# Three experts instead of two gathered by rank, and the second half of the slot gather placed behind the third gate/up product

## The reference

```python
def hier_moe(h, w_rg, b_rg, w_re, b_re, w_gate, w_up, w_down):
    ...
    gate = grp_p[:, None] * jax.nn.softmax(top_val, axis=-1)
    expert = grp[:, None] * MOE_EXPERTS_PER_GROUP + top_idx
    ...
    def run_block(args):
        xb, e = args
        hid = jax.nn.silu(xb @ w_gate[e]) * (xb @ w_up[e])
        return hid @ w_down[e]

    ys = lax.map(run_block, (xs, blk_expert)).reshape(n_slots, D)
    out = jnp.zeros((T + 1, D), jnp.float32).at[slot_tok].add(
        ys.astype(jnp.float32) * slot_gate[:, None])[:T]
```

## Time and profile before

| | us |
|---|---|
| median of 3 runs | 1012.68 (1011.05 to 1013.63) |
| the profiled execution | 1009.09 |
| its span in the trace | 1007.3 |
| PE busy | 928.9 (92%) |
| DVE busy | 277.3 (28%) |
| ACT busy | 205.7 (20%) |
| POOL busy | 184.3 (18%) |

### The profile page before, as it was taken

The page is one execution under the profiler, slowest core; times in us unless marked ns, Lnnn a source line. Parts: engine busy times, 40 slices in busy tenths (PEclk is TensorE's granted clock), DMA queues, the critical chain, the costliest instruction groups (busy, mean ns, idle before and its releaser), DMA issues.

```text
span 1007.3 us, 13643 instructions
## 1 busy us (share of the span) xinstructions
PE 928.9 (92%) x5416; PEld 555.1 (55%) x5416; DVE 277.3 (28%) x732; ACT 205.7 (20%) x483; POOL 184.3 (18%) x307
## 2 busy tenths in 40 slices
PE   5899898999999999888898889799999889999886
PEld 4788686554444434343343334587677448488632
DVE  2399633411110011100100110233353145042214
ACT  2354323310000000000000000311126311012630
POOL 0177200121111111110110110001012102013313
PEclk8999999999999999999999999999999999999998
DMA  9995864589999999999999999922002942302001
GB/s 371 430 427 218 365 273 176 243 319 428 426 427 429 429 426 429 427 426 428 428 426 427 429 426 430 420 91 112 18 2 115 396 168 84 132 35 85 1 1 42
DMA packets 21949, 286.17 MB, mean 284 GB/s; under 512 B 2434, under 2 KB 3202, under 8 KB 4354
## 3 DMA queue, kind: packets, MB, share of 16 engines
q1 hardware_dynamic: 21168, 283.99, 67.7%
q10 hardware_dynamic: 722, 1.33, 0.3%
HBM read 284.26 MB, written 1.05 MB: 283 GB/s over the span
## 4 chain that ended last, share of the span: by engine, by line
PE 69%; DMA 24%; DVE 2%; POOL 2%; issue 1%; ACT 1%; SPq 1%; POOLq 0%; ACTq 0%; DVEq 0%
DMA arena<-in_w_expert_up 21%; PE bank L914 20%; PE bank L1122 14%; PE bank L1291 6%; PE bank L1139 5%; DMA arena<-in_w_glu 3%; PE bank L1254 3%; PE bank L1401 3%; PE bank L1149 3%; PE bank L1278 2%; PE bank L1110 1%; PE bank L981 1%; PE bank L1268 1%; PE bank L933 1%; PE bank L1325 1%
## 5 line engine op out<-in xcount | busy, mean ns | idle before, releaser
L1122 PE MATMUL bank<-arena 128*64 128x512 f32 x1024 | 226.1, 593 | 24.7 <-DMA arena<-in_w_expert_up 24.7
L914 PE MATMUL bank<-arena 128*128 128x256 f32 (+1 forms) x912 | 203.4, 384 | 6.8 <-ACT arena L788 4.3
L914 PEld LDWEIGHTS bank<-arena 128*128 128x128 f32 (+1 forms) x912 | 173.6, 191 | 34.6 <-issue 6.9
L1122 PEld LDWEIGHTS bank<-arena 128*64 128x64 f32 x1024 | 79.4, 137 | 167.8 <-issue 167.6
L1139 PE MATMUL bank<-arena 128*64 128x512 f32 x512 | 116.9, 598 | 0.8 <-ACT arena L758 0.8
L1700 DVE TENSOR_TENSOR arena<-bank,arena 64x512 f32<-64x512 f32 x32 | 21.8, 682 | 280.1 <-ACT arena L754 280.1
L758 ACT ACTIVATE arena<-bank 128x512 f32<-128x512 f32 x32 | 19.1, 598 | 387.1 <-PE bank L1131 387.1
L1139 PEld LDWEIGHTS bank<-arena 128*64 128x64 f32 x512 | 34.1, 136 | 65.8 <-issue 65.8
L1149 PE MATMUL bank<-arena 64*128 64x256 f32 x512 | 65.8, 386 | 0.8 <-DVE arena L1703 0.8
L533 POOL COPY der<-arena 128x4 f32 (+1 forms) x30 | 5.6, 187 | 319.3 <-PE bank L1131 297.8
L1506 DVE SCALAR_TENSOR_TENSOR bank<-arena,par,bank 128x256 f32<-128x256 f32 x152 | 61.9, 483 | 0.6
(11 more groups left out here) (237 smaller groups left out, 847.2 us busy)
## 6 DMA issues: line engine op xcount, KB each, us to landing
arena<-in_w_expert_gate SPq DMA_DIRECT2D x32, 2048.0 KB, 27.1
arena<-in_w_expert_up SPq DMA_DIRECT2D x32, 2048.0 KB, 31.5
arena<-in_w_expert_down SPq DMA_DIRECT2D x32, 2048.0 KB, 30.8
arena<-in_w_ada SPq DMA_DIRECT2D x11, 2048.0 KB, 30.0
arena<-in_w_glu SPq DMA_DIRECT2D x4, 2048.0 KB, 34.8
arena<-in_w_kv SPq DMA_DIRECT2D x4, 2048.0 KB, 18.9
arena<-in_w_in_b SPq DMA_DIRECT2D x4, 2048.0 KB, 7.9
arena<-in_w_uq SPq DMA_DIRECT2D x4, 1152.0 KB, 13.9
```

Source lines behind the costliest of these rows:

```text
L914: mm = pe.matmul(bank[part:part + m, at:at + n], w[:, k, lo:lo + m], rhs[:, k0 + k, :], start=(k == 0), stop=(k == tiles - 1))
L1122: mm = pe.matmul(GU_BANK[half * WIN:(half + 1) * WIN, :], xw[b][:, k, :], w[:, k, :], start=(k == 0), stop=(k == KD - 1), skip_group_check ...
```

## The change

The gather by rank now covers three experts (BODY): DVE builds selectors of 192 columns instead of 128, the 16 matmuls are 192 columns wide instead of 128, and ACT moves 128 x 192 instead of 128 x 128. POOL prepares the weighting of experts 0, 1 and 2 at once (`first_window`) and no longer copies a window for expert 2.

The second half of the slot gather moves from behind gate/up 1 to behind gate/up 2. In between now stand the turn and down product of expert 0. The bank table follows: half 0 uses banks 1 to 7 from bank 1 on, half 1 uses banks 3 to 7. There are two waits for moves on PE as before, but each now stands directly behind a gather: for banks 1 to 3 behind half 0, ahead of gate/up 1, and for banks 4 to 7 behind half 1, ahead of finish(2). The turned buffer of expert 0 moves out of the memory of `sel`. ACT and DVE get the matching order.

```diff
-        for half in range(2):
-            for j in range(KD):
-                plan(("gather", half, j), 1 + (KD * half + j + 5) % 7)
+        for j in range(KD):
+            plan(("gather", 0, j), 1 + j % 7)
+        BEFORE_GATHER = list(reads)
+        for j in range(KD):
+            plan(("gather", 1, j), 3 + j % 5)
...
-            first_window(0)
-            first_window(1)
+            for e in range(BODY):
+                first_window(e)
             for half in range(2):
                 for j in range(KD):
                     moved(pool, ("gather", half, j))
-            window(2, 0, 2, win_ready)
...
-                    mm = pe.matmul(bank[:, 0:2 * WIN], h2_tok[:, t, j * P:(j + 1) * P], first_sel[:, t, :],
+                    mm = pe.matmul(bank[:, 0:BODY * WIN], h2_tok[:, t, j * P:(j + 1) * P], first_sel[:, t, :],
...
-                if e < 2:
-                    gather(e)
+                if e == 0:
+                    gather(0)
+                    for b in range(1, 4):
+                        pe.wait_ge(sem(f"bank{b}_read"), BEFORE_GATHER[b])
+                if e == 2:
+                    gather(1)
+                    for b in range(4, 8):
+                        pe.wait_ge(sem(f"bank{b}_read"), BEFORE_EXPERTS[b])
                 if e:
-                    for b in range(1, 4) if e == 1 else range(4, 8):
-                        pe.wait_ge(sem(f"bank{b}_read"), BEFORE_EXPERTS[b])
                     finish(e, e, lambda s, back: EXPERT_BASE[s] + 16, second=e == 1, third=e == 2)
...
-            for half in range(2):
-                for j in range(1, KD, 2):
-                    gathered(half, j)
-            with dve.Fori(1, EXPERTS) as e:
+            for j in range(1, KD, 2):
+                gathered(0, j)
+            dve.wait_ge(silu_done, 2)
+            dve.wait_ge(t_full, 1 + C_T)
+            gated(hid_ready)
+            dve.wait_ge(y_full, 1)
+            move_result(y_moved)
+            for j in range(1, KD, 2):
+                gathered(1, j)
+            with dve.Fori(2, EXPERTS) as e:
```

More of the change, by code:

```diff
@@ L143, in two_blocks @@
         wr2 = area(R + 6144, KD, CHOICES)
-        first_sel = area(R + 6144, NT, 2 * WIN)
+        first_sel = area(R + 6144, NT, BODY * WIN)
         shift_row, shift_all = small[0:1, 940:940 + CHOICES], small[:, 900:900 + CHOICES]
@@ L151, in two_blocks @@
         xw = [area(R + 4608 + b * KD * WIN, KD, WIN) for b in range(BODY)]
-        first_xw = arena[:, R + 4608:R + 4608 + 2 * KD * WIN].rearrange("p (e k n) -> p e k n", e=2, k=KD)
+        first_xw = arena[:, R + 4608:R + 4608 + BODY * KD * WIN].rearrange("p (e k n) -> p e k n", e=BODY, k=KD)
         weighted = [area(R + 12288 + b * NT * P, NT, P) for b in range(BODY)]
@@ L155, in two_blocks @@
         hid = arena[0:WIN, R + 6144:R + 6144 + HIDDEN]
-        turned_e = [arena[:, R + 10240 + b * 512:R + 10752 + b * 512] for b in range(BODY)]
+        turned_e = [arena[:, at:at + 512] for at in (R + 11264, R + 10240, R + 10752)]
         hid_t = [a[:, 0:KF * WIN].rearrange("p (f n) -> p f n", f=KF) for a in turned_e]
@@ L742, in _ @@
                 bank = filled(act, name)
-                act.activation(first_xw[:, :, j, :], bank[:, 0:2 * WIN].rearrange("p (e n) -> p e n", e=2), ACT.Identity,
+                act.activation(first_xw[:, :, j, :], bank[:, 0:BODY * WIN].rearrange("p (e n) -> p e n", e=BODY), ACT.Identity,
                                bias=mod[:, 24 + j:25 + j], scale=a2[:, j:j + 1]).then_inc(read(name), 1)
@@ L763, in _ @@
             silu(gu_full, 2, silu_done)
+            move_turned(t_full, C_T + 1, 0, t_moved)
+            silu(gu_full, 3, silu_done)
             for j in range(0, KD, 2):
                 gathered(1, j)
[L766 to L769, removed]
+            move_turned(t_full, C_T + 2, 1, t_moved)
+            silu(gu_full, 4, silu_done)
+            move_turned(t_full, C_T + 3, 2, t_moved)
             with act.Fori(1, LOOPS) as it:
@@ L1640, in _ @@
             iota = rc[:, R_IOTA:R_IOTA + SLOTS_A]
-            first_rank = tmp(990, NT, 2)
-            then(dve.scalar_tensor_tensor(out=first_rank, in0=bank[:, 0:64].rearrange("p (t e) -> p t e", t=NT)[:, :, 0:2],
-                                          scalar=1.0, in1=picked[:, :, 0:2], op0=ALU.add, op1=ALU.mult))
+            first_rank = tmp(990, NT, BODY)
+            then(dve.scalar_tensor_tensor(out=first_rank, in0=bank[:, 0:64].rearrange("p (t e) -> p t e", t=NT)[:, :, 0:BODY],
+                                          scalar=1.0, in1=picked[:, :, 0:BODY], op0=ALU.add, op1=ALU.mult))
             for t in range(NT):
-                dve.tensor_tensor(first_sel[:, t, :].rearrange("p (e n) -> p e n", e=2),
-                                  iota[:, 1:WIN + 1].unsqueeze(1).broadcast_to((P, 2, WIN)),
-                                  first_rank[:, t, :].unsqueeze(2).broadcast_to((P, 2, WIN)), ALU.is_equal) \
+                dve.tensor_tensor(first_sel[:, t, :].rearrange("p (e n) -> p e n", e=BODY),
+                                  iota[:, 1:WIN + 1].unsqueeze(1).broadcast_to((P, BODY, WIN)),
+                                  first_rank[:, t, :].unsqueeze(2).broadcast_to((P, BODY, WIN)), ALU.is_equal) \
                     .then_inc(sem("first_sel"), 1)
```

## The result

| | before | after |
|---|---|---|
| median of 20 runs each, us | 1011.08 (1006.38 to 1013.63) | 1013.83 (1009.43 to 1016.57) |
| ratio, 95% interval | | 1.0031 (1.0020 to 1.0043) |
| the profiled execution, us | 1009.09 | 1016.17 |
| its span | 1007.3 | 1014.4 |
| PE busy, us | 928.9 | 936.5 |

The change costs 3.1 us, between 2.0 and 4.3. The two medians differ by 2.75 us. The prediction had +1.3. A second timing of the changed kernel, beside the first experiments, gave 1.0025 (1.0006 to 1.0043).

The account below looks back on a forecast made before the run. The weight DMA queue's last dry moment was taken to bound the expert stage. Wider gather 1.6 and two waits of 0.65 make 2.9, less 1.6 margin, +1.3 us: 1014.0 us from the 1012.68 median, range 1010.8 to 1017.5.

Parts of the forecast that it names:

- The bound and the last dry moment: Expert stage: it ends by the weight queue's last dry moment, at 221 us before, at the expert 6 pair after, +1.3.
- the margin: Expert 6 pair: before the change it was issued 1.6 us ahead of the weight queue running dry.
- Wider gather by rank: First gather on PE: 64 more columns in each of 32 records cost 1.6 us, bounds 1.2 to 2.0.
- if the clock rises at the same moment this holds wherever the columns stand: First gather: with an unchanged clock rise, the added columns cost 1.8 us before overlap with weight loads, wherever they stand.
- The two waits: PE behind gather halves 0 and 1: waiting for DVE's last move costs 0.65 us each, bounds 0.5 to 0.8.
- Half 1 moved for nothing: Second slot gather half, 7.0 us on PE: leaves ahead of down 0, returns ahead of turn 1, nothing in total.
- the 0.78 us stays: PE between turn 0 and down 0: the existing 0.78 us wait for ACT remains.
- POOL is covered: POOL's window of expert 3: ready 3.2 us after half 1 is moved, some 3 us to spare.
- The sum: Whole path: 2.9 us of added delay less 1.6 us of margin makes +1.3 us.
- The queue does run dry again: Weight queue: forecast a new dry spot near 237 us; the rival without one claimed -4.3 us, 1008.4, 6%.
- PE's new costs don't show: PE, gathers: no wait behind them and wider columns hidden by weight loads, -1.6 us, 1011.1; rival, 8%.
- The clock stays low through the first gather: First gather: half clock throughout makes it 10.7 us, +5.5 instead of +1.6, total +5.2, 1017.9; rival, 8%.

Follow-up runs that it names:

- e3: Kernel before plus seven extra matmuls of 256 columns, result unread, on PE ahead of gate/up of expert 3; 1.0008 (0.9984 to 1.0032).
- e4: Kernel before plus seven extra matmuls of 256 columns, result unread, on PE ahead of gate/up 0; 1.0032 (1.0015 to 1.0049).
- e7: Changed kernel plus six extra matmuls in PE's idle time around the rank matmuls; median 1009.94 us, 0.9995 (0.9968 to 1.0022) against the kernel before.
- e8: Kernel before plus six extra matmuls in PE's idle time around the rank matmuls, second run; median 1007.94 us, 0.9974 (0.9953 to 0.9994).
- after_again: Changed kernel once more without any edit, as control and second trace; 1.0025 (1.0006 to 1.0043) against the kernel before.
- before_again: Kernel before once more, unchanged, for a third trace; 443.18 us from first gather to last gate/up product, no whole time given.
- e2_late_waits: Changed kernel with both PE waits for moved banks later, ahead of turn 0 and behind turn 1; 0.9997 (0.9970 to 1.0024) against the kernel before.
- e1_wide_only: Kernel before with only the gather by rank widened to three experts and without POOL's window for expert 2; 1.0028 (1.0003 to 1.0054).

## Why the prediction was right in kind and short in size

The direction, the mechanism and the range held. That 1013.83 us came so close to 1014.0 is luck: the median of before was 1.6 us lower over 20 runs than over the 3 shown, and the difference of the two kernels was +3.1 us (2.0 to 4.3) and not +1.3, two errors that nearly cancel. The forecast's own bounds for the difference, +0.6 to +2.0, only touch the measured interval. Step by step:

- **The bound and the last dry moment.** Right. The queue was dry last at the pair for expert 5 before, and is at the pair for expert 6 after. e3 and e4 show that only delays ahead of that moment count in full, and that the margin behind it is 1.6 us.
- **Wider gather by rank, +1.6 us.** This is the mis-sized term. At equal clock it is exactly that, 5.44 - 3.81 = 1.63 (e7, e8). But in the traces without the extra matmuls it was 2.35 and 2.1 (after, after_again), above my upper bound of 2.0. The step "if the clock rises at the same moment this holds wherever the columns stand" has its condition in it, and that condition didn't hold: the rise came 3.0 us after the gather's start before and 4.4 after. Half of 1.4 us is the missing 0.7.
- **Whose are those 0.7 us?** They go with the moment at which the clock fell, not with the width. The table has all eight traces without the extra matmuls. Fall and rise are counted from the start of the gather by rank, from the granted clock in stretches of half a us; the last column runs from the first rank matmul to gate/up 0.

| trace | fall ahead, us | rise behind, us | gather, us | rank matmuls and gather, us |
|---|---|---|---|---|
| before (narrow) | 3.8 | 3.0 | 5.23 | 8.25 |
| before_again (narrow) | 3.8 | 3.1 | 5.26 | 8.28 |
| e3_delay_third (narrow) | 0.1 | 3.3 | 5.38 | 7.35 |
| e4_delay_first (narrow) | 2.2 | 4.6 | 6.00 | 8.53 |
| e2_late_waits (wide) | 3.2 | 3.7 | 7.24 | 10.33 |
| after_again (wide) | 2.9 | 3.9 | 7.37 | 10.34 |
| after (wide) | 2.5 | 4.4 | 7.58 | 10.35 |
| e1_wide_only (wide) | 1.7 | 5.1 | 7.94 | 10.37 |

The fall always came before the gather, so the gather's width can't have placed it. In seven of the eight traces, narrow and wide, the clock then stayed low for 6.8 us, so a later fall meant a later rise and a longer gather; e3 is the exception. Where fall and rise lie nearly alike (e4 and after), the wide one takes 1.6 us more, as at full clock. What puts the fall where it is isn't shown, nor whether the changed kernel makes a late one likelier. A late fall also gives something back, which the interval leaves out: more of the rank matmuls ahead then run at the full level. Counted from the first rank matmul to the last gate/up product the two traces of the change are 2.2 and 1.7 us longer than the first of before, where the interval had 2.45 and 1.76. The Trainium skill ("TensorE: Matmul & The Clock Gate", part 1, "What's actually happening") has the point of the rise vary by some 500 ns either way; counted from the gather's start it varied by more here, between 3.0 and 5.1 us.

- **The two waits, 0.65 us each.** They are there, with 0.64 and 0.68 us of idle time. The first is released by DVE's move as foreseen; the second has no releaser in the trace, but it ends with DVE's move and is gone in e2, where the wait stands elsewhere. On the path they are 0.7 and 0.85: without a wait the record of the next product starts 0.07 us before that of the gather ends (before, 194.96 against 187.86 + 7.17), and that overlap goes too. I took the idle time of the nearest row as the price; together that missed 0.25.
- **Half 1 moved for nothing, the 0.78 us stays, POOL is covered.** Right. The window of expert 3 was copied by 230.5 us and gate/up 3 began at 232.9, 2.4 us to spare where I had 3.
- **The sum.** With the two corrections (+0.75 and +0.25) the 2.9 us become 3.9, which is what the issue of the pair for expert 6 is late by (3.94); less the margin of 1.58 that is +2.4, and the interval grew by 2.45. The mean of both traces of the change over both of before is +2.2. What is left to the 3.1 or 2.5 of the whole times is within their intervals.
- **The rivals.** The queue does run dry again, so the 4.3 us were not to be had. "PE's new costs don't show" fell with the visible gaps. "The clock stays low through the first gather" didn't happen, but it was the right place to worry about: a milder form of it, a rise 1.4 us later, is what was missing in the sum. I had given it a full price and 8% and nothing in between.

Behind the numbers stands why the change doesn't pay: bringing half 1 behind gate/up 2 removes two dry spots, worth at most the 1.6 us of margin to the next one, and what is new on PE's path, 1.6 us for the wider gather and 1.55 for the two waits, is paid ahead of that next one.

## What to carry to other kernels

Where a queue with a fixed order of issues is the bound, look for the last moment at which it is dry: work moved past it is worth only the distance to the next issue that could come late, and delays ahead of it count in full. A wait for buffers belongs directly ahead of the instruction that overwrites them; two waits placed a step too early were 1.55 of the 3.9 us that this change added ahead of the last dry moment. And before making matmuls wider or fewer at a place where the clock has fallen, try to fill the idle time ahead of them: here six matmuls that nobody reads gained 2.3 and 2.6 us in two timings, where the change lost 3.1.

## What was not expected of the hardware

The clock fell although PE's longest pause in the ten us ahead of the gather by rank was 2.0 us (2.03 in the trace of e4_delay_first, ahead of the rank matmuls). Six matmuls of 0.44 us in those pauses kept it at the full level in all four traces that had them; in all eight without them it fell, at the latest 0.1 us ahead of the gather. The gain over the kernel before is plain: 1.4 us in the gather by rank and 1.0 between the first rank matmul and the gather.

Nor was it expected that the clock's part in the gather by rank would be set before it starts: in seven of the eight traces the clock rose the sooner the earlier it had fallen, 3.0 us into the gather after a fall 3.8 us ahead of it and 5.1 us into it after a fall 1.7 us ahead.
